# A convolution layer's input products: high and low halves of the rows in one product of 512 columns

## The reference

```python
def conv_mixer(x, w_in, conv_w, w_out):
    b, c, u = jnp.split(x @ w_in, 3, axis=-1)
    z = lax.conv_general_dilated(c * u, conv_w[:, None, :], window_strides=(1,),
                                 padding=[(CONV_WIDTH - 1, 0)],
                                 dimension_numbers=('NWC', 'WIO', 'NWC'),
                                 feature_group_count=D_MODEL)
    return (b * z) @ w_out
```

## Time and profile before

| | |
|---|---|
| median of 3 executions | 1846.87 us (1846.51 to 1847.53) |
| the profiled execution, its own time | 1846.83 us |
| its span, first to last instruction | 1845.0 us |
| mean granted TensorE clock | 0.999 |
| TensorE busy | 1827.9 us, 99% of the span |
| VectorE busy | 1111.8 us, 60% |
| ScalarE busy | 924.1 us, 50% |
| GpSimd busy | 574.9 us, 31% |
| the convolution layer's six input projections | about 1213 to 1282 us of the span |

### The profile page before, as it was taken

The page is one execution under the profiler, slowest core; times in us unless marked ns, Lnnn a source line. Parts: engine busy times, 40 slices in busy tenths (PEclk is TensorE's granted clock), DMA queues, the critical chain, the costliest instruction groups (busy, mean ns, idle before and its releaser), DMA issues.

```text
span 1845.0 us, 25464 instructions
## 1 busy us (share of the span) xinstructions
PE 1827.9 (99%) x10104; PEld 1579.1 (86%) x10104; DVE 1111.8 (60%) x1995; ACT 924.1 (50%) x1099; POOL 574.9 (31%) x128
## 2 busy tenths in 40 slices
PE   9999999999999999999999999999999999999998
PEld 7888888889998988888888888899888889888887
DVE  7887789886777895222867322666522287952226
ACT  7655556455554544444454444444444445454443
POOL 0000000000000007787002888300787700068870
PEclk9999999999999999999999999999999999999999
DMA  9534434644244346555433655455655543365551
GB/s 367 183 137 174 169 137 160 214 160 180 93 160 143 115 174 219 198 190 184 180 148 143 220 190 182 160 184 211 229 186 199 185 162 136 142 229 192 195 186 65
DMA packets 53193, 326.60 MB, mean 177 GB/s; under 512 B 8640, under 2 KB 11072, under 8 KB 15584
## 3 DMA queue, kind: packets, MB, share of 16 engines
q1 hardware_dynamic: 45472, 311.54, 46.3%
q10 hardware_dynamic: 7616, 13.59, 2.3%
HBM read 324.07 MB, written 1.05 MB: 176 GB/s over the span
## 4 chain that ended last, share of the span: by engine, by line
PE 93%; DVE 3%; ACT 2%; DMA 1%; issue 1%; SPq 0%; ACTq 0%; DVEq 0%
PE project L1192 37%; PE output L1192 31%; PE turn L1612 5%; PE project L1612 5%; PE project L1618 2%; PE turn L1618 2%; PE turn L1428 2%; PE output L1521 1%; PE output L1393 1%; PE output L1368 1%; PE turn L1347 1%; DMA arena<-in_ln_b 1%; PE output L1376 1%; DMA raw<-in_units 1%; DVE arena L2229 0%
## 5 line engine op out<-in xcount | busy, mean ns | idle before, releaser
L1151 POOL TENSOR_TENSOR wlo<-raw,whi 128x2048 fp32r<-128x2048 f32 x124 | 574.7, 4666 | 1221.6 <-ACT whi L1681 1204.8
L1681 ACT ACTIVATE whi<-raw 128x2048 fp32r<-128x2048 f32 x289 | 546.9, 1910 | 336.1 <-PE project L1612 166.1
L1192 PE MATMUL project<-whi,XT 128*128 128x512 f32 x1376 | 450.0, 397 | 2.3 <-DVE arena L2248 1.2
L2090 DVE TENSOR_TENSOR wlo<-raw,whi 128x2048 fp32r<-128x2048 f32 x165 | 375.1, 2286 | 21.9 <-ACT whi L1681 21.2
L1192 PEld LDWEIGHTS project<-whi,XT 128*128 128x128 f32 x1376 | 258.5, 188 | 56.3 <-issue 3.2
L1192 PE MATMUL output<-whi,YTh 128*128 128x512 f32 x736 | 288.4, 392 | 1.5 <-DVE YTl L2631 1.5
L1192 PE MATMUL output<-whi,YTl 128*128 128x512 f32 x736 | 287.1, 390 | 0.0
L1192 PE MATMUL output<-wlo,YTh 128*128 128x512 f32 x736 | 286.9, 390 | 0.0
L1192 PE MATMUL project<-wlo,XT 128*128 128x512 f32 x688 | 268.1, 390 | 0.0
L2925 DVE TENSOR_TENSOR arena<-project,arena 128x256 f32<-128x256 f32 x48 | 20.4, 425 | 408.9 <-ACT arena L2046 408.9
L1192 PE MATMUL project<-XT,whi 128*128 128x256 f32 x1184 | 219.0, 285 | 0.0
(11 more groups left out here) (292 smaller groups left out, 2311.4 us busy)
## 6 DMA issues: line engine op xcount, KB each, us to landing
raw<-in_units SPq DMA_DIRECT2D x290, 1024.0 KB, 4.8
arena<-in_ln_g ACTq DMA_DIRECT2D x8, 512.0 KB, 5.4
arena<-in_ln_b ACTq DMA_DIRECT2D x8, 512.0 KB, 6.9
xres<-in_x SPq DMA_DIRECT2D x2, 1024.0 KB, 10.5
raw<-in_units SPq DMA_DIRECT2D x2, 512.0 KB, 7.2
tok<-in_mem SPq DMA_DIRECT2D x1, 1024.0 KB, 14.3
arena<-in_x_t SPq DMA_DIRECT2D x1, 1024.0 KB, 18.1
arena<-in_mem_t ACTq DMA_DIRECT2D x1, 1024.0 KB, 4.7
```

The source lines that it names most:

```text
L1151: pool.tensor_tensor(wlo[:, slot, :], raw[:, slot, :], whi[:, slot, :], ALU.subtract).then_inc(lo_pool, 1)
L1192: mm = pe.matmul(out, x if x_stationary else w, w if x_stationary else x, start=start and i == 0, stop=stop and i == 2, skip_group_check=True)
L1681: act.activation(whi[:, slot, :], raw[:, slot, :], ACT.Copy).then_inc(hi_done, 1)
L2090: dve.tensor_tensor(wlo[:, slot, :], raw[:, slot, :], whi[:, slot, :], ALU.subtract).then_inc(lo_dve, 1)
```

## The change

Five of the six projections take the MLP's form (`wide=True`); cc of pass 0 stays as it was. `wide_unit` on TensorE uses the banks PP and PT; the first wide projection waits for the last two uses of PT as transpose banks, and `wait_bank`, in front of the next transpose, for the last wide projection's banks. ScalarE copies the right halves of a bank pair (`right_halves_of`), VectorE adds the left halves to them (`add_halves`). For cu and cb the multiplications by cc and cz now follow the additions, from SBUF. With `low_last=True` a wide projection's additions (and multiplications) stand in front of the low half that its second unit carries. The taps are a step of their own, behind this low half and in front of cb's first unit. In cb ScalarE's part for bank pair 0 is: copies, wait for the product with cz, high half; then the same for pair 1.

```diff
@@ conv
-            project(("conv_w_in", 0), 1024 + j * 512, "cc", feature_major=True)
-            project(("conv_w_in", 0), 2048 + j * 512, "cu", feature_major=True, j=j)
-            project(("conv_w_in", 0), j * 512, "cb", feature_major=True, j=j)
+            project(("conv_w_in", 0), 1024 + j * 512, "cc", feature_major=True, wide=j == 1, low_last=j == 1)
+            project(("conv_w_in", 0), 2048 + j * 512, "cu", feature_major=True, j=j, wide=True, low_last=True)
+            add("taps", j=j)
+            project(("conv_w_in", 0), j * 512, "cb", feature_major=True, j=j, wide=True, low_last=True)
@@ TensorE
+            def wide_unit(n, slot, g, u, t):
+                wait_lo(pe, n)
+                if u == 0 and not wide_last:
+                    wait_bank(t)
+                    wait_bank(t + 1)
...
+                for m in range(4):
+                    b, ms = m // 2, slice(m * P, (m + 1) * P)
+                    bank = (PP, PT)[m % 2][b]
+                    if u == 0 and m % 2 == 0:
+                        pe.wait_ge(p_evac[b], g)
+                    for k in range(4):
+                        mm = pe.matmul(bank[:, :], wh[:, k, ms], XT[:, 4 * u + k].rearrange("p a s -> p (a s)"),
+                                       start=u == 0 and k == 0, stop=False, skip_group_check=True)
...
+                    for k in range(4):
+                        mm = pe.matmul(bank[:, S:2 * S], wl[:, k, ms], XTh[:, 4 * u + k, :], start=False,
+                                       stop=u == 1 and k == 3, skip_group_check=True)
+                    if u == 1 and m % 2 == 1:
+                        mm.then_inc(p_done[b], 1)
@@ ScalarE
+            def right_halves_of(part, b, g):
+                act.wait_ge(p_evac[b], g)
+                act.wait_ge(p_done[b], g + 1)
+                act.activation(part[:, 2 * b, :], PP[b][:, S:2 * S], ACT.Copy).then_inc(act_own, 1)
+                last.own()
+                act.activation(part[:, 2 * b + 1, :], PT[b][:, S:2 * S], ACT.Copy).then_inc(wide_ready, 1)
...
+                    elif tag == "cu":
+                        right_halves_of(cu, b, g)
...
                     elif tag == "cb":
+                        right_halves_of(cy, b, g)
                         act.wait_ge(v2a, nth("v2a"))
@@ VectorE
+            def add_halves(part, b, g):
+                dve.wait_ge(wide_ready, nth("wide"))
+                for x, bank in enumerate((PP[b], PT[b])):
+                    ins = dve.tensor_tensor(part[:, 2 * b + x, :], bank[:, 0:S], part[:, 2 * b + x, :], ALU.add)
+                    if x:
+                        ins.then_inc(p_evac[b], 1)
...
                 elif tag == "cu":
                     for b in range(2):
-                        dve.wait_ge(p_evac[b], g)
-                        dve.wait_ge(p_done[b], g + 1)
+                        add_halves(cu, b, g)
                         x = slice(2 * b, 2 * b + 2)
-                        dve.tensor_tensor(cu[:, x, :], cc[:, x, :], PP[b][:, :].rearrange("p (a s) -> p a s", a=2),
-                                                     ALU.mult).then_inc(p_evac[b], 1)
+                        dve.wait_ge(*last.at)
+                        dve.tensor_tensor(cu[:, x, :], cc[:, x, :], cu[:, x, :], ALU.mult).then_inc(dve_own, 1)
...
                 elif tag == "cb":
                     for b in range(2):
-                        dve.wait_ge(p_done[b], g + 1)
+                        add_halves(cy, b, g)
                         x = slice(2 * b, 2 * b + 2)
-                        dve.tensor_tensor(cy[:, x, :], cz[:, x, :], PP[b][:, :].rearrange("p (a s) -> p a s", a=2),
-                                                     ALU.mult).then_inc(p_evac[b], 1)
                         dve.wait_ge(*last.at)
-                        dve.tensor_copy(st[:, 95:96], st[:, 94:95]).then_inc(v2a, 1)
+                        dve.tensor_tensor(cy[:, x, :], cz[:, x, :], cy[:, x, :], ALU.mult).then_inc(v2a, 1)
```

More of the change, by code:

```diff
@@ L1328, in wait_bank @@
             def wait_bank(t):
+                if wide_last:
+                    g = wide_last.pop()
+                    for b in range(2):
+                        pe.wait_ge(p_evac[b], g + 1)
                 if t >= 2:
@@ L1443, in _ @@
                             wait_turned("B", whole=f["u"] == 1)
+                    if f.get("wide"):
+                        wide_unit(f["n"], f["n"] % RING, f["g"], f["u"], f["t"])
+                        continue
                     xs = (YTh, YTl) if f["src"] == "M" else (XTh, XTl)
@@ L1702, in load_gla @@
                     load(small, a["c_small"], pos_in)
+            def right_halves_of(part, b, g):
[4 more added lines that the diff above has]
+                act.activation(part[:, 2 * b + 1, :], PT[b][:, S:2 * S], ACT.Copy).then_inc(wide_ready, 1)
+                last.other(wide_ready, nth("wide"))
             def square_of(f, b, buf, sq):
@@ L1755, in post @@
                         copy_bank(b, g, dst[:, x:x + 2, :].rearrange("p a s -> p (a s)"))
+                    elif tag == "cc" and f["wide"]:
+                        right_halves_of(cc, b, g)
+                    elif tag == "cu":
+                        right_halves_of(cu, b, g)
                     elif tag == "cc":
@@ L2317, in post @@
                         last.other(qk_ready, nth("qk"))
+                elif tag == "cc" and f["wide"]:
+                    for b in range(2):
+                        add_halves(cc, b, g)
                 elif tag == "cu":
                     for b in range(2):
-                        dve.wait_ge(p_evac[b], g)
-                        dve.wait_ge(p_done[b], g + 1)
+                        add_halves(cu, b, g)
                         x = slice(2 * b, 2 * b + 2)
-                        dve.tensor_tensor(cu[:, x, :], cc[:, x, :], PP[b][:, :].rearrange("p (a s) -> p a s", a=2),
-                                                     ALU.mult).then_inc(p_evac[b], 1)
@@ L2331, in post @@
                     dve.wait_ge(*last.at)
[L2332 to L2339, removed]
@@ L2355, in post @@
                         last.other(conv_lo, 2 * f["j"] + b + 1)
+            def add_halves(part, b, g):
[4 more added lines that the diff above has]
+                        ins.then_inc(p_evac[b], 1)
+                        last.other(p_evac[b], g + 1)
+                    else:
+                        ins.then_inc(dve_own, 1)
+                        last.own()
             def stage_of(stage, i):
@@ L2633, in _ @@
                     last.other(t_evac[t % 2], t // 2 + 1)
+                elif kind == "taps":
+                    for m in range(4):
+                        k = 4 * f["j"] + m
+                        dve.tensor_scalar(cz[:, m, :], cu[:, m, :], convw[:, k, 2:3], None, ALU.mult).then_inc(dve_own, 1)
+                        last.own()
+                    dve.wait_ge(*last.at)
+                    for w in (1, 0):
+                        d = 2 - w
+                        for m in range(4):
+                            k = 4 * f["j"] + m
+                            dve.scalar_tensor_tensor(out=cz[:, m, d:], in0=cu[:, m, :S - d], scalar=convw[:, k, w:w + 1],
+                                                        in1=cz[:, m, d:], op0=ALU.mult, op1=ALU.add).then_inc(dve_own, 1)
+                            last.own()
+                        dve.wait_ge(*last.at)
                 elif kind == "post":
```

27 lines of the change are left out of this document (15 added, 12 removed).

## The result

The changed kernel takes 1852.49 us (median of 8 executions, 1851.14 to 1852.96), the kernel before 1846.89 us in the same session (8, 1846.45 to 1848.16): ratio 1.0028, interval 1.0019 to 1.0037. It is slower, by 0.3%, clear of the noise. The forecast was 1850.7 in a range of 1848.9 to 1852.9: right in its sign, 1.8 us short in its size. The profiled execution took 1852.7 us.

What follows compares the result with a forecast made beforehand. TensorE, busy 99% of the span, was taken as the bound. Wide units gain 1.6 us, waits for VectorE lose 2.67 in pass 0 and 2.84 in pass 1: +3.9 us, 1850.7, range 1848.9 to 1852.9.

Steps and rivals of the forecast that it cites:

- Gain on TensorE: Convolution layer: ten of twelve weight units become wide, 5.60 us each instead of 5.76, gaining 1.6 us.
- Rival 2: Wide units take 5.76 us like narrow ones, so nothing is gained on TensorE: +5.5 us, 1852.4; chance 0.06.
- rival 1: Low halves 5 and 11 still made while VectorE waits for cu, chains 2.21 us shorter: 1846.3, not slower; chance 0.08.
- low half of unit 5: VectorE's preparation of weight unit 5 in pass 0, now behind cu's additions; forecast in time for its unit.
- T: End of cu's second unit (unit 3) in pass 0, from which the forecast counts its VectorE steps.
- The chain on VectorE: VectorE's queue from cu's additions to low halves 7 and 13: losses of 2.67 us in pass 0, 2.84 in pass 1.
- low half of 7: VectorE's last preparation in pass 0's chain: unit 7 begins at T + 19.47 instead of T + 16.80, 2.67 us lost.
- all four: TensorE stops forecast before units 6, 7, 12 and 13: about 1.1, 1.5, 0.5 and 2.3 us.
- The forecast's own interval: The forecast without its rivals, 1849.9 to 1852.0 us, given a chance of 0.80.
- The sum: Gain of 1.6 us against losses of 2.67 and 2.84 us: +3.9 us, 1850.7.
- the third rival: TensorE's clock falls to 1.2 GHz behind unit 13's stop: up to 5.4 us more, 1856.1; chance 0.04.
- the stop of 2.35 us: TensorE's wait before unit 13, in pass 1, for that unit's low half; forecast longer than any stop before.

Runs made afterwards that it cites:

- the better order: All products wide as in the change, but low halves 5, 6, 11, 12 made while VectorE waits for cu, 7 and 13 before cb's additions: 1845.18 us, ratio 0.9992.
- Pass 0 alone: Wide products everywhere; pass 0 in the changed kernel's order, pass 1 with low halves made early while VectorE waits for cu: 1848.10 us, ratio 1.0006.
- pass 1 alone: Wide products everywhere; pass 1 in the changed kernel's order, pass 0 with low halves made early while VectorE waits for cu: 1848.42 us, ratio 1.001.
- its stops filled: Changed kernel plus four, six and ten 512-column products into a bank nobody reads, in the stops before units 6, 7 and 13: 1850.96 us, ratio 1.0022.
- unshifted changed kernel: The change as is; its shifted version issues one 512-column product far ahead of the layer eleven times instead of once: 1854.74 us, ratio 1.0040.

## Why the prediction was right and where it was short

**Gain on TensorE: right.** 5.61 us for a wide unit against 5.60; the kernel with the better order gains 1.7 us in the median, for 1.6. Rival 2 (no gain) is out, though its time, 1852.4, is by chance the one measured: only the units' length in the trace tells the two apart. So is the shorter chain of rival 1: it would have put the low half of unit 5 while VectorE waited for cu; it started at T + 2.47.

**The chain on VectorE: right, step by step.** Forecast and trace, from T: low half of 5 at 2.42 and 2.47, taps 4.63 and 4.68, low half of 6 9.21 and 9.25, additions 11.42 and 11.46, of pair 1 14.19 and 14.18, low half of 7 17.00 and 16.97. No step is off by more than 0.05; no stop was where none was forecast in the layer, and all four were where they were. By the weight loads they were 1.15, 1.32, 0.43 and 2.43 us, for 1.1, 1.5, 0.5 and 2.3.

**Each part by an undo: right.** Pass 0 alone +2.9 for 2.67, pass 1 alone some +3.0 for 2.84, and the layer's whole 3.95 for 3.9. With its stops filled the changed kernel takes 1850.96, and the forecast was 1850.7.

**What was luck.** The forecast's own interval was 1849.9 to 1852.0, and 1852.49 lies above it. It lies in the range only since the range reaches up to 1852.9 for rival 2, which is out. The sum is short by a term that it put at nothing.

**What failed: the third rival's chance and size.** The prediction said that the wait of 1.46 us "kept 1.00", and from that one execution took it that the clock holds; a fall behind the stop of 2.35 us got a chance of 0.04 and a price of up to 5.4 us. The runs show the reverse: 13 of 16 executions of the changed kernel are long, both of the profiled ones by a fall of the clock, and the one at 575 us cost 1.6 us (36 products in 10.0 us for 8.4). In it the products stand further apart for some 3.4 us, not for a unit. The missing 1.8 us of the median is mostly this term: with the three stops filled, and the order as it was, 1.5 us of them are gone. The one profile and the three executions of before that the prediction had (1846.51 to 1847.53) did not show it, though that profile's trace holds a granted clock of 0.75 at 1842 to 1844, where TensorE has no products left and it costs nothing; over 101 executions the kernel before has two clusters of times, some 1.5 us apart (below 1847.6 and above 1847.7), and two executions at 1851.4 and 1851.5.

The sum was thus made for an execution without a fall, while the median of the changed kernel is most likely one with a fall; the kernel before goes without in two of three.

## What to carry to other kernels

Where one engine is the bound, work put on another is free only as long as each piece of it stands before it is asked for: write that engine's queue down in order, with times, before moving a step behind another, and move what is ready early (here the low halves of weights) into the time in which it waits anyway. The same wide products cost 3.9 us in the layer in one order and gained 1.7 us in another. When a change makes new idle stretches of TensorE, look at all executions and not at one profile: clusters of times can be a sign that a clock falls in some of them. A few products into an unused bank, put into the stops, show whether it does.

## What was not expected of the hardware

TensorE's clock fell to 0.50 behind idle times of 1.46 us (575) and 2.05 us (unit 13), in some executions and not in others of the same program, with the same idle time to 0.01 us; behind the stop of 1.43 to 1.45 us at 934 no trace has a fall. The fall at 575 cost about 1.6 us. No execution of the unshifted changed kernel was longer by two falls (the longest is 2.3 us above the shortest), though it has both places. And VectorE took 5.69 us for 1.42 us of work while GpSimd ran, behind a load for which it had waited 1.1 us longer.
